# A ring of seven row buffers instead of eight in the decode stage, with one gate-weight tile loaded during chunk compression

## The reference

```
(qa, ck, cv, sk, sv, wk, wv, ng, fq, fk, fv, logf, ga, gb) = project(rms_norm(x), p)
o_cmp, o_sel = nsa_cmp_sel(qa, qpos, cat(c_cmp_k, ck), cat(c_cmp_v, cv), cat(c_sel_k, sk), cat(c_sel_v, sv), p)
o_win = window_attend(qa, qpos, wk_all, wv_all, kpos_w)      # 512 rows of state_win_k, state_win_v
o_fox = fox_attend(fq, qpos, c_new, (cached fox_k, fox_v, ...), (fk, fv, ...))
o_a = ng[..., 0:1] * o_cmp + ng[..., 1:2] * o_sel + ng[..., 2:3] * o_win
ya, yb = o_a @ w_o_a, o_fox @ w_o_b
h = x + (sigmoid(ga) * ya + sigmoid(gb) * yb) @ w_out
y = h + conv_ffn(h)
```

## Time and profile before

| | |
|---|---|
| median of 3 runs | 894.61 us (894.05 to 895.12) |
| the profiled execution's own time | 897.77 us |
| its span in the trace | 896.0 us |
| TensorE matmul busy | 834.1 us (93%) |
| VectorE, ScalarE, GpSimd busy | 508.3, 366.7, 182.8 us |
| data moved | 192.07 MB |

### The profile page before, as it was taken

How to read it: one execution, slowest core, us unless ns; L and a number is a source line. 1 busy time by engine, 2 the same in 40 slices (tenths; PEclk the granted TensorE clock), 3 DMA queues, 4 the chain that set the end, 5 groups by cost and what they waited for, 6 DMA issues and landing times. The chain is left out here.

```text
span 896.0 us, 18498 instructions
## 1 busy us (share of the span) xinstructions
PE 834.1 (93%) x7479; PEld 683.8 (76%) x7479; DVE 508.3 (57%) x972; ACT 366.7 (41%) x660; POOL 182.8 (20%) x276
## 2 busy tenths in 40 slices
PE   6999688999999999999998788999899999999997
PEld 4999556889889876647554458996599889889885
DVE  6477577433436677644566425636756556656654
ACT  5256656333344144532243405435154344344332
POOL 3000377200320123233343500000011101101010
PEclk9999879899999999999999998999989999999999
DMA  5643494922345399999999988863074445554412
GB/s 203 196 145 120 78 334 176 233 108 95 119 159 196 128 401 341 343 408 411 419 417 395 398 325 224 228 244 120 0 235 142 141 143 193 187 180 140 140 47 64
DMA packets 90645, 192.07 MB, mean 214 GB/s; under 512 B 7467, under 2 KB 68812, under 8 KB 78061
## 3 DMA queue, kind: packets, MB, share of 16 engines
q0 software_dynamic: 15408, 106.04, 30.5%
q1 hardware_dynamic: 74878, 84.05, 30.3%
q10 hardware_dynamic: 288, 0.97, 0.3%
HBM read 187.57 MB, written 7.64 MB: 218 GB/s over the span
## 5 line engine op out<-in xcount | busy, mean ns | idle before, releaser
L1760 PEld LDWEIGHTS banks<-consts_base,stream_rows 128*128 128x128 f32 x672 | 73.1, 141 | 33.5 <-issue 26.9
L1999 ACT ACTIVATE keys_turned<-banks 128x512 f32<-128x512 f32 x94 | 55.1, 597 | 99.0 <-PE banks L1760 98.8
L1760 PE MATMUL banks<-consts_base,stream_rows 128*128 128x128 f32 x672 | 82.7, 276 | 6.9 <-DVE fox_probs_turned L1990 2.6
L261 PE MATMUL banks<-tokens_turned_high,w_gates_high 128*128 128x288 f32 x288 | 86.6, 301 | 2.3 <-PEq L194 2.3
L262 PE MATMUL banks<-tokens_turned_low,w_gates_high 128*128 128x288 f32 x288 | 85.6, 297 | 0.0
L263 PE MATMUL banks<-tokens_turned_high,w_gates_low 128*128 128x288 f32 x272 | 81.8, 301 | 0.0
L1293 PE MATMUL banks<-chunks_turned_high,cmp_w_high 64*128 64x256 f32 (+1 forms) x512 | 77.4, 296 | 2.6 <-ACT cmp_hidden L1387 2.6
L1293 PE MATMUL banks<-chunks_turned_low,cmp_w_high 64*128 64x256 f32 (+1 forms) x512 | 74.2, 284 | 0.0
L1980 DVE COPY keys_turned<-banks 128x512 f32<-128x512 f32 x74 | 50.4, 690 | 33.5 <-PE banks L1760 31.0
L254 DVE TENSOR_TENSOR chunks_turned_low<-banks,chunks_turned_high 128x512 fp32r<-128x512 f32 x64 | 41.1, 684 | 43.0 <-ACT chunks_turned_high L249 43.0
L249 ACT ACTIVATE chunks_turned_high<-banks 128x512 fp32r<-128x512 f32 x64 | 34.8, 596 | 68.4 <-PE banks L1136 66.2
(11 more groups left out here) (458 smaller groups left out, 2106.4 us busy)
## 6 DMA issues: line engine op xcount, KB each, us to landing
w_up_gate<-in_w_up SPq DMA_DIRECT2D x12, 1024.0 KB, 7.4
w_up_gate<-in_w_gate SPq DMA_DIRECT2D x12, 1024.0 KB, 9.9
w_down<-in_w_down SPq DMA_DIRECT2D x12, 1024.0 KB, 5.1
w_in_slot<-in_w_in SPq DMA_DIRECT2D x7, 1424.0 KB, 7.8
w_gates<-in_w_in SPq DMA_DIRECT2D x10, 512.0 KB, 6.8
cmp_w_k<-in_cmp_w_k SPq DMA_DIRECT2D x4, 512.0 KB
cmp_w_v<-in_cmp_w_v SPq DMA_DIRECT2D x4, 512.0 KB, 10.8
stream_rows<-in_state_win_k SPq DMA_DIRECT2D x8, 256.0 KB, 9.3
```

The lines of the kernel that those rows point to most:

```text
L261: nc.tensor.matmul(out, lh, rh, start=start, stop=False, **kw)
L1760: ins = nc.tensor.transpose(bank(t)[:, q * P:(q + 1) * P], src, ident)
L1999: copy = lambda a, b: nc.scalar.activation(a, b, ACT.Copy)
```

## The change

`DEC_RING` becomes 7. Buffers: 0 to 3 as before, buffer 4 in the bridge at 24K, buffers 5 and 6 in what compress leaves. The tile `gates` moves to the bridge's bytes 16K to 24K; SP loads it at the end of its list in `stage_compress`, once half of the compression steps are used. Its load in POOL's decode loop goes. The gather of item 5 is issued in decode, not in compress. ACT waits for the last key products before `split(1)`, because the high part is written over `keys_turned`. `w_out_high0` and `w_out_low0` of the merge move to the new place of `gates`.

```diff
@@ stage_compress, SP and POOL
             chunks.load_w1(sp, 1)
+            sp.wait_ge(used, NSTEP // 2)
+            load_gates(c, sp, c.gates, c.gates_in, P)
...
             pool.wait_ge(used, NSTEP // 2)
-            for n in (4, 5, 0, 1, 2, 3):
+            for n in (4, 0, 1, 2, 3):
...
-DEC_RING = 8
+DEC_RING = 7
@@ stage_decode, SP
-            release(sp, ring.index(last_in(5)))
+            release(sp, ring.index(last_in(4)))
             load_wo(c, sp, c.wo, c.wo_in, 0)
@@ stage_decode, POOL
-            for n in range(6, len(ring)):
+            for n in range(5, len(ring)):
                 if n == ring.index(("vals", "fox", 1, 1)) + R:
                     pool.wait_ge(turned, last_turn(("probs", "fox", 1, 4)))
                     load_gates(c, pool, c.gates1, c.gates1_in, 0)
-                if n == ring.index(("keys", "nsa", 1, 4)) + R + 1:
-                    pool.wait_ge(products, done[last_key])
-                    load_gates(c, pool, c.gates, c.gates_in, P)
@@ stage_decode, ACT
                         act.wait_ge(nsa_taken, 14)
+                    if i == 1:
+                        act.wait_ge(products, done[last_key])
@@ stage_merge
-offset=(c.bridge_at, wg1_at)[k] + n * 4 * D
+offset=(c.bridge_at + 16 * KD * P, wg1_at)[k] + n * 4 * D
@@ build
-        c.gates = c.at("w_gates0", [P, 2, KD, P], F32, 0)
-        c.gates_high, c.gates_low = (c.at(f"w_gates_{x}0", [P, 2, KD, P], F32R, 8 * KD * P * (n + 1)) for n, x in enumerate(("high", "low")))
+        c.gates = c.at("w_gates0", [P, 2, KD, P], F32, 16 * KD * P)
+        c.gates_high, c.gates_low = (c.at(f"w_gates_{x}0", [P, 2, KD, P], F32R, 8 * KD * P * n) for x, n in (("high", 1), ("low", 0)))
...
-            c.stream += [c.at(f"stream_rows{n}", [P, CS * KVW], F32, 4 * (n - 2) * CS * KVW) for n in (4, 5)]
+            c.stream.append(c.at("stream_rows4", [P, CS * KVW], F32, 4 * 3 * CS * KVW))
...
-            c.stream += [c.sb(f"stream_rows{n}", [P, CS * KVW], ctx=mid) for n in (6, 7)]
+            c.stream += [c.sb(f"stream_rows{n}", [P, CS * KVW], ctx=mid) for n in (5, 6)]
```

More of the change, by code:

```diff
@@ L2303, in stage_merge @@
         one = lambda x: x[:, :, :, :].rearrange("p a j e -> p (a j e)")
-        early = [[nc.alloc_sbuf_tensor_at(f"w_out_{x}{k}", [P, D], F32R, offset=(c.bridge_at, wg1_at)[k] + n * 4 * D)[:, :]
+        early = [[nc.alloc_sbuf_tensor_at(f"w_out_{x}{k}", [P, D], F32R, offset=(c.bridge_at + 16 * KD * P, wg1_at)[k] + n * 4 * D)[:, :]
                   for n, x in enumerate(("high", "low"))] for k in range(2)]
@@ L2892, in build @@
         c.sb("bridge", [P, 4 * 2 * KD * P])
-        c.gates = c.at("w_gates0", [P, 2, KD, P], F32, 0)
-        c.gates_high, c.gates_low = (c.at(f"w_gates_{x}0", [P, 2, KD, P], F32R, 8 * KD * P * (n + 1)) for n, x in enumerate(("high", "low")))
+        c.gates = c.at("w_gates0", [P, 2, KD, P], F32, 16 * KD * P)
+        c.gates_high, c.gates_low = (c.at(f"w_gates_{x}0", [P, 2, KD, P], F32R, 8 * KD * P * n) for x, n in (("high", 1), ("low", 0)))
         c.wo = c.at("w_o0", [P, 2, 4, P], F32, 24 * KD * P)
         c.wo_high = c.at("w_o_high0", [P, 2, 4, P], F32R, 28 * KD * P)
-        c.gates_low_here, c.wo_low_here = c.at("w_gates_low_in_place", [P, 2, KD, P], F32R, 0), c.at("w_o_low_in_place", [P, 2, 4, P], F32R, 24 * KD * P)
+        c.gates_low_here, c.wo_low_here = c.at("w_gates_low_in_place", [P, 2, KD, P], F32R, 16 * KD * P), c.at("w_o_low_in_place", [P, 2, 4, P], F32R, 24 * KD * P)
         c.gates_in, c.wo_in, c.gates1_in = c.sem("w_gates_in0"), c.sem("w_o_in0"), c.sem("w_gates_in1")
```

## The result

The changed kernel takes 900.25 us (median of 6 runs, 899.32 to 903.2) against 894.33 us (6 runs, 891.39 to 896.88): ratio 1.0065, 95% interval 1.0047 to 1.0084, so about 5.9 us slower. Run again beside the experiments it took 901.58 (median of 7) against 895.14, ratio 1.0065 (1.0044 to 1.0085); an eighth execution of that run took 1620.2 us and is left out. The forecast of 897.0 and its range up to 899.4 were too low. The profiled execution took 899.32 us with a span of 897.5.

The account below looks back on a forecast made before the run. Keys part paced by PE; afterwards DMA engines are full and PE runs nearly level with them. Terms 2.8 + 1.2 - 2.6 + 1.0 = +2.4 us put the median at 897.0 us, range 894.2 to 899.4.

Parts of the forecast that it names:

- Item 57: +2.8: Window keys in decode: SP's load, released by item 50 and not 49, makes PE wait 2.8 us more.
- The slow stretch of the clock: Rival, chance 0.11: after 3.9 us of idling at item 57 PE runs at half clock, 1.7 us more, 898.7.
- Item 69: +1.2: Window item in decode: load goes out 2.2 us later, less 1.0 of assumed slack, so 1.2 us more wait.
- The gates load: -2.6: Late decode: without the second gate tile's load, waits of 1.36 and 1.24 us at items 75 and 76 go.
- both waits are gone: Items 75 and 76: item 75 lands near 510.8, PE comes at 514.5, so waits of 1.36 and 1.24 vanish.
- the tile costs nothing in compress: Compress: the moved gate tile takes item 5's place with the same megabyte, PE has landed items, cost nothing.
- w_o: +1.0: End of decode: w_o's load waits for item 81 and not 77, delaying the merge by 1.0 us, ends 0 and 2.35.
- L: Time from SP's second w_o issue to its landing, taken as 3.9 us; the cost at w_o is L - 2.85.
- signs of a wrong forecast: No growth of item 57's wait, a gathered item waiting over 2 us before item 72, or over 0.5 us change before 440.
- The rival "faster": Chance 0.10: window loads speed up, item 57's to 15.0 us or less, no lag forms, -2.1 us, 892.5.

Follow-up runs that it names:

- the filled wait: The changed kernel with 28 transposes of the identity put ahead of PE's wait for item 57: 901.13 us.
- after_again: The changed kernel run once more with no edit, beside the experiments: 901.58 us, ratio 1.0065 to the kernel before.
- after_win_lead1: The changed kernel, seven places, with window items from item 32 on given their places one turn ahead: 895.24 us, ratio 1.0009.
- lead1_not_item69: The changed kernel with places one turn ahead for window items 32 and 57 only, item 69 as changed: 897.28 us, ratio 1.0023.

## Why the prediction was wrong

The mechanism was in the main the forecast one: SP's window loads, released one item later, make PE wait. Three steps of the sum failed. Item 32 was priced at nothing, the stretch at half clock behind item 57 was left out of the sum, and item 69 was priced as if its load would still take the 15.1 us of before. Besides, the gain at items 75 and 76 was put down to the wrong cause.

*Item 32: not priced, the step that was missed.* Its load too is released one item later, which was 1.0 us here. In the trace of before its last packet ended at 401.97, 1.2 us ahead of the use, but no wait on DMA stood there, and I had looked for waits on DMA only. PE starts 0.7 to 0.9 us after a last packet, so 0.4 us of that was cover. Measured lag there: 1.2, 1.6, 3.6 and 1.0 us in the four traces with seven places and the release of the change; 0, 0, 0.9 and 1.2 in four with SP's loads and eight places (one of them with the later release, whose load was quick). So some 1 to 1.5 us, and not all of it the change's: the time of this load to its last packet varies by itself, from 15.1 to 17.4 us where no more than one turn of lead was given. The 3.6 us hold a stretch at half clock, from 404.9 on.

*Item 57: +2.8, right.* +2.9 and +3.0 us in the two traces of the changed kernel; from issue to landing the load took 18.1 and 18.2 us, for 17.9 before.

*The slow stretch of the clock: a rival at 0.11, it came.* In all four traces with 3.6 to 4.2 us of wait ahead of item 57 the granted clock fell to 0.50 in the wait's last 1.2 us or within 1.2 us behind it, for 3.4 or 6.8 us; there in none of the others. It costs 1.6 to 2.8 us, in the changed kernel's two traces 1.8 and 1.5. I had set it low since DVE was to hide it; it did not. In the changed kernel DVE idled again among its next rows, 1.11 and 0.22 us where the kernel before has no gap, and its own lag grew from 4.4 us at its first row behind item 57 to 5.8 us at the probabilities that PE waits for near 475. The Trainium skill (TensorE: Matmul & The Clock Gate, HAM oscillation) says that waits for DMA throttle PE anew; the traces agree, and it deserved more than a ninth.

*Item 69: +1.2, mis-sized.* The lag grew by 0 in one trace of the changed kernel and by 4.9 us in the other, by 4.6 in the run that moved the other two windows, by 6.8 behind the filled wait. The release was sized right: it adds 2.2 us in every trace that has it. So was the slack: the load of before ended at 494.45, the use was at 496.03, PE starts some 0.8 us after a last packet, which leaves 0.8. What failed is the tacit step that the load takes the 15.1 us of before. To its last packet it took 12.9 and 17.0 us in the two traces of the changed kernel and 10.9 to 18.2 in all with the later release. With these the sum from the rows works: 2.2 - 0.8 + (17.0 - 15.1) = 3.3 us for a wait of 3.19, and 2.2 - 0.8 + (18.2 - 15.1) = 4.5 for 4.20. The rest of the 4.9 and 6.8 us, 1.7 and 2.6 us, goes with a stretch at half clock that follows in both traces.

One thing that makes this load slower is that it goes out later. In the kernel before, the first gate tile's load ran beside it; SP's load that goes out 8.1 us later finds that tile landed. SP's whole load lies in these stretches, 483 to 494 before, 488 to 500 in after_again (packets, MB, share of 16 engines):

```profile
q0 software_dynamic: 561, 3.05, 74.2%
q1 hardware_dynamic: 557, 1.02, 28.5%
```

```profile
q0 software_dynamic: 532, 3.86, 78.0%
q1 hardware_dynamic: 567, 1.03, 23.0%
```

POOL's queue has as many packets as SP's in both, but before nearly half of them are the tile's, of 4 KB, and later all are gathers', of 8 KB, so each turn of SP's queue takes longer. By the packets of all twelve traces in which SP issued this load, it took 14.7 to 15.3 us in the four with some 250 of the tile's packets beside it, and 17.0 to 18.2 us in the four with fewer than 40 and a POOL queue that never emptied. The tile's new place ahead of item 68 is not what parts them: after_win_lead1 has it there too, with SP's load as early as before, and 252 of the tile's packets stand beside it; in lead1_not_item69, where SP's load goes out 2.1 us later, there are 160, and it took 16.9 us. No run changed what runs beside this load and nothing else, so what the tile is worth in the time is not shown.

*The gates load: -2.6, right in size, wrong in cause.* The lag fell by 2.9 us in both traces. It does so with the gates load left in place as well. By my own working item 75 would have landed at 511.8 + 2.5 = 514.3 with the load left in place, and PE came at 514.5: the waits were gone without the removal. So the step "both waits are gone" holds, the reason "without it" does not, and at the place where I had booked it the removal was, behind such a lag, worth nothing. That the tile costs nothing in compress was right: from 200 to 383 us no trace shifts by more than 0.03 us against that of the kernel before.

*w_o: +1.0, it was about 0.6 to 0.7.* L was 3.5 and not 3.9. The Trainium skill's fit for one DMA (DMA: Bandwidth & Descriptors, Anatomy of one DMA), which the Trainium skill gives for GpSimd's path while w_o goes out on SP's, would have made it 0. The run of this part alone can't tell the two apart (ratio 0.9986 to 1.0017); the rows of the merge can, and they stand between.

With these sizes: 1.2 + 2.9 + 1.8 + 0 - 2.9 + 0.7 - 0.7 = 3.0 for the first trace (item 32, item 57, clock, item 69, repaid, w_o, clock stretches after decode), and 1.6 + 3.0 + 1.5 + 4.9 - 2.9 + 0.6 - 1.2 = 7.5 for the second, which ended 7.6 us late. These are readings of the same traces that they are to explain; that the parts are what I take them for rests on the runs above, and the stretches after decode were not tested. One of my own signs of a wrong forecast, over 0.5 us of change before 440, is there; the others (no growth at item 57, a gathered item waiting over 2 us before item 72) are not.

What stays open: from one trace to the next the program reaches decode 0.8 to 5.2 us sooner than in the trace of the kernel before. The difference arises between 100 and 180 us, where the stretches at half clock fall differently; no run separates the clock from what else may differ there. From 95 to 170 us, in the kernel before and in the one without the gates load, whose instructions are the same up to decode:

```profile
95.00:170.00 75.00, 58.11 (x487) 44.24 (x485) 46.66 (x186) 41.24 (x133) 43.01 (x76) 0.82 0.72 209
```

```profile
95.00:170.00 75.00, 56.68 (x550) 43.71 (x548) 49.40 (x188) 43.10 (x136) 45.57 (x80) 0.93 0.78 217
```

A granted clock of 0.82 against 0.93. With eight places the decode stage began on average 3.0 us earlier than in the first trace of before (6 traces), with seven 2.3 us (8 traces), so up to 0.7 us of the loss may lie there; I can't say that it does. And the traces don't show how often item 69 waits in the changed kernel: the 5.9 us is a mean over executions that differ by over 4.

## What to carry to other kernels

When a ring is shortened, look at every load that goes through another queue than the rest, not only at those that wait already: its lead shrinks by one item too, and here these loads had 0.4 and 0.8 us of cover, or none. Who gets a place when is worth as much as how many places there are: one turn of lead for three loads gave back all that the eighth place was worth, while three turns cost as much as the change. A wait that a change removes must be asked for with the lag that the same change makes: if PE comes later anyway, the wait is gone for free and can't be booked a second time. A load's own time is not a constant of the load: ask what runs beside it, before the change and after. And a wait on DMA that grows to 4 us should be priced with the half-speed stretch behind it.

## What the runs showed of the hardware

The 1 MB load of a window by SP's queue took, to its last packet, from 7.1 us (the first window keys of the changed kernel, issued at 328.28, where PE sets the pace) to 18.2 us (item 69 behind the filled wait). The rows of DMA queues in the changed kernel (packets, MB, share of 16 engines) show why. First 451 to 460, within item 57's load, then 491 to 492, within item 69's:

```profile
q0 software_dynamic: 412, 3.00, 80.7%
q1 hardware_dynamic: 410, 0.75, 22.0%
```

```profile
q1 hardware_dynamic: 216, 0.39, 104.1%
q0 software_dynamic: 4, 0.01, 2.2%
```

In the first stretch the two queues get the same number of packets, 412 and 410, and so four fifths of the bytes go to POOL's of 8 KB and one fifth to SP's of 2 KB. The Trainium skill (DMA: Bandwidth & Descriptors, Queues, rings and completion order) says that each engine goes round between its queues packet by packet; this trace agrees. It makes the load's time a sum: 3.5 us from SP's issue to its first packet, and then the bytes of both queues at the engines' full rate. From the first packet at 450.64 to the last at 464.55 SP's queue moved 1.05 MB and POOL's 4.69 MB, 5.74 MB in 13.9 us, together 17.4 us. Over the whole load POOL's queue so got some more turns than SP's; 512 packets of each would have been 5.2 MB and, at the same 414 GB/s, 16.2 us. Item 57's load took 17.0 to 17.5 us in all twelve traces in which SP issued it. In the second stretch POOL's queue had run dry and SP's load had the engines to itself, 0.39 MB in 1 us. A load of this kind so takes a long time beside a queue that is never empty, fixed by the size of that queue's packets, and by an estimate from these rows each us in which that queue is empty saves it some four (0.39 MB in 1 us, for 0.08 beside the gathers): item 69's took 12.9 us here. That can explain why its time differs between two traces of the same kernel, 12.9 and 17.0 us; what made POOL's queue run dry in one and not in the other is not shown. The rival "faster" asked for such a gap at item 57; with seven places POOL's queue never ran dry there.
